# SBUF addresses of the weight rings and work regions: rings allocated last, one buffer padded from 392 to 512 bytes

## The chip, the cores and the metric

One core of one Trainium2 chip runs the whole program once. The metric is the device time of that execution in microseconds; lower is better. Each kernel is timed several times and the median is compared.

## What is computed

Two transformer-like blocks of two layers each, in float32, on one sequence of 256 tokens with 1024 features. The weights are each read once from HBM. Cut to what matters:

```python
# first block, DEPTH = 2
for layer in range(2):
    h = rms_norm(x, norm_mix[layer])
    x = x + hybrid_mixer(h, w_in[layer], ...)      # nine 1024x1024 projections, recurrence, conv, three more
    h = rms_norm(x, norm_ffn[layer])
    x = x + (swiglu(h, dense_w1, dense_w3, dense_w2) if layer == 0
             else moe_swiglu(h, router_w, expert_w1, expert_w3, expert_w2))   # 8 experts, top 2
x = rms_norm(x, final_norm)
# second block, DEPTH = 2
for l in range(2):
    x = x + 0.5 * rmsnorm(swiglu_ffn(rmsnorm(x, ...), ffn1_w_gu[l], ffn1_w_down[l]), ...)
    x = x + rmsnorm(mixing_sublayer(rmsnorm(x, ...), w_in[l], ...), ...)
    x = x + 0.5 * rmsnorm(swiglu_ffn(rmsnorm(x, ...), ffn2_w_gu[l], ffn2_w_down[l]), ...)
```

Every feed-forward has width 2816. An expert works on at most 128 gathered tokens, every other product on all 256.

## The kernel before, in words

All large weights are laid out ahead of time as one stream of **slabs**, each 128 partitions by 2048 float32 (1 MB). A slab goes through three rings of three slots each (`RING = 3`): SyncE's queue writes it from HBM into `raw` in two halves (`Sync.slabs`, L265), ScalarE rounds each half to float32r into `whi` (`Scalar.hi`, L301), VectorE computes the rest `wlo = raw - whi` (`Vector.lo`, L726), and TensorE multiplies (`Tensor.slab`, L1289 to L1291). The other operand is split in the same way into a high and a low part, and three products stand for one float32 product:

```python
            pe.matmul(ps, xh, k.whi[:, slot, cols], start=first, stop=False)
            pe.matmul(ps, xh, k.wlo[:, slot, cols], start=False, stop=False)
            mm = pe.matmul(ps, xl, k.whi[:, slot, cols], start=False, stop=last)
```

The first argument behind `ps` is the stationary operand (a weight load of 128 columns, 512 bytes a partition); the slab is the operand that streams past it, 512 columns or 2048 bytes a partition. Each of the three has a weight load of its own. So in the rows a matmul `ps<-whi,XH` streams `whi` past the stationary `XH`.

The stationary operands come in two places. `XH` and `XL` (the transposed, normalised input of a mixer or of a feed-forward's first product, for 256 tokens) are buffers of their own. `GH`/`GL` (the gated hidden activations, for the down product of a dense feed-forward), `GH_`/`GL_` (the same for an expert) and `XEH`/`XEL` (an expert's gathered input) lie in `region_z`, one region of 73,728 bytes a partition that the stages reuse by turns with different layouts. `region_b` is another such region, with the mixers' tables (`mcum`, L1387 and L1388, streams past `LFH` and `LFL`).

A slot of `raw` is written again once VectorE has read it; a slot of `whi` and `wlo` is written again once TensorE is done with its slab (the semaphores `dve_lo` and `pe_slab`). The order on every engine is written out in the code. In the down stage of an expert TensorE also gathers the next expert's tokens between slabs. The stages: mixer, dense feed-forward, mixer, the eight experts (each 22 slabs for the first products, the "up" stage, and 11 for the second, the "down" stage), then for each layer of the second block a feed-forward, a mixer, a feed-forward.

`Tiles.memory` allocates the buffers. Addresses are given out in the order of the calls, each rounded up to 32 bytes, beginning at byte 16,512 of each partition.

Of the kernel before, what the change touches and what calls it, by code (L numbers as in the profile page):

```python
# [8 lines left out]
F32R = mybir.dt.float32r  # L9
# [7 lines left out]
P = 128  # L17
# [20 lines left out]
SLAB = 2048  # L38
HALF = SLAB // 2
RING = 3  # L40
# [6 lines left out]
PCOLS = 2 * LCOLS + 2 * KT  # L47
# [11 lines left out]
class Tiles:  # L59
# [52 lines left out]
        return made  # L112

    def memory(self):
        self.raw = self.sb("raw", [P, RING, SLAB])
        self.whi = self.sb("whi", [P, RING, SLAB], F32R)
        self.wlo = self.sb("wlo", [P, RING, SLAB], F32R)
        self.X = self.sb("X", [P, NT, D])
        self.XN = self.sb("XN", [P, NT, D])
        self.XH = self.sb("XH", [P, KT, S], F32R)  # L120
        self.XL = self.sb("XL", [P, KT, S], F32R)
        self.ident = self.sb("ident", [P, P])
        self.small = self.sb("small", [P, 192])
        self.pcols = self.sb("pcols", [P, PCOLS])

        b = self.overlays("region_b", 6816, [
            ("mcum", [P, 12 * P], F32R),
            ("masks", [P, 7, P], U8),
            ("E1", [P, NT, 8, P], F32),
            ("KQ", [P, 2, 2 * S], F32),  # L130
            ("LFH", [P, 2, NT, P], F32R), ("LFL", [P, 2, NT, P], F32R),
            ("SM", [P, 2, NT, P], F32), ("SC", [P, 2, P], F32),
            ("ones1", [P, P], F32),
        ], [
            ("pad", [P, 3808], F32), ("mload", [P, 12 * P], F32), ("mask_load", [P, 7, P], F32),
        ], [
            ("RB", [P, NT, 4, S], F32),
            ("MP", [P, 4, 3 * P], F32),
            ("WS", [P, 4, P], F32),
            ("PW", [P, 4, 64], F32),  # L140
            ("pc2", [P, PC2], F32),
            ("gvb", [P, BW], F32),
            ("ones", [P, P], F32),
            ("GP", [P, D], F32),
        ], [
            ("pad2", [P, 4834], F32), ("bias_tmp", [P, 1028], F32),
        ])
        self.mcum, self.masks, self.E1, self.KQ, self.LFH, self.LFL, self.SM = (b[n] for n in ("mcum", "masks", "E1", "KQ", "LFH", "LFL", "SM"))
        self.SC, self.mload, self.RB, self.MP, self.WS, self.PW, self.pc2 = (b[n] for n in ("SC", "mload", "RB", "MP", "WS", "PW", "pc2"))
        self.gvb, self.ones, self.ones1, self.mask_load, self.GP, self.bias_tmp = (b[n] for n in ("gvb", "ones", "ones1", "mask_load", "GP", "bias_tmp"))  # L150

        n = 9 * SEG
        z = self.overlays("region_z", n, [("Z", [P, n], F32)], [
            ("GH", [P, FT, S], F32R), ("GL", [P, FT, S], F32R),
            ("SG", [P, 3, NT, S], F32), ("GN", [P, 3, NT, S], F32),
        ], [
            ("GH_", [P, FT, P], F32R), ("GL_", [P, FT, P], F32R),
            ("SG_", [P, 3, S], F32), ("GN_", [P, 3, S], F32),
            ("XEH", [P, KT, P], F32R), ("XEL", [P, KT, P], F32R),
            ("PM", [P, NT, P], F32),  # L160
            ("PT", [P, S], F32R),
            ("YH", [P, D], F32R), ("YL", [P, D], F32R),
            ("GB", [P, D], F32), ("RW", [P, KT, NE], F32), ("RWH", [P, KT, NE], F32R), ("RWL", [P, KT, NE], F32R),
            ("iota_", [P, P], F32), ("iota", [P, P], F32), ("ltri", [P, 3, P], F32), ("mo", [P, 512], F32),
        ], [
            ("Z2", [P, 12 * NT * CW], F32),
            ("HP", [P, 2, 30 + S], F32), ("CA", [P, 2, S], F32), ("CB", [P, 2, S], F32),
            ("QT", [P, 2, S], F32), ("KTT", [P, 2, S], F32), ("QI", [P, 2, S], F32),
            ("LG", [P, 4, S], F32), ("SCO", [P, 2, S], F32), ("WRK", [P, 2, S], F32), ("m8", [P, 16], F32),
        ])  # L170
        self.Z, self.GH, self.GL, self.SG, self.GN, self.GH_, self.GL_ = (z[n] for n in ("Z", "GH", "GL", "SG", "GN", "GH_", "GL_"))
        self.SG_, self.GN_, self.XEH, self.XEL, self.PM, self.PT, self.YH = (z[n] for n in ("SG_", "GN_", "XEH", "XEL", "PM", "PT", "YH"))
        self.YL, self.GB, self.RW, self.RWH, self.RWL, self.iota_, self.iota = (z[n] for n in ("YL", "GB", "RW", "RWH", "RWL", "iota_", "iota"))
        self.ltri, self.mo, self.Z2, self.HP, self.CA, self.CB, self.QT = (z[n] for n in ("ltri", "mo", "Z2", "HP", "CA", "CB", "QT"))
        self.KTT, self.QI, self.LG, self.SCO, self.WRK, self.m8 = (z[n] for n in ("KTT", "QI", "LG", "SCO", "WRK", "m8"))
        self.ps = self.stack.enter_context(self.nc.psum_tensor("ps", [P, 8, CW], F32))

        sm = self.small
        self.eps, self.rsin, self.nrs = sm[:, 0:1], sm[:, 20:22], sm[:, 24:26]
        self.ss, self.rs = sm[:, 8:10], sm[:, 16:18]  # L180
        self.oss, self.orn = sm[:, 32:48], sm[:, 48:64]
        self.gslot = sm[:, 64:65]
        self.lb_a = self.pcols[:, PCOLS - 2 * KT:PCOLS].rearrange("p (l c) -> p l c", l=2)
        self.lb_e, self.lb_s = sm[:, 128:144].rearrange("p (l c) -> p l c", l=2), sm[:, 120:128]
        self.lb = sm[:, 104:120].rearrange("p (l c) -> p l c", l=2)
# [1593 lines left out]
class Pool(Engine):  # L1779


    def start(self):
        pool, k = self.eng, self.k
        pool.dma_start(k.pcols[:], k.a["pcols"]).then_inc(*k.up("d_pcols", "pcols", 16))
        pool.memset(k.ident[:], 0.0).then_inc(*k.up("pool_step", "ident0"))
        pool.wait_ge(*k.at("ident0"))
        pool.affine_select(out=k.ident[:], in_=k.ident[:], compare_op=ALU.not_equal, fill=1.0, base=0, pattern=[[-1, P]],
                           channel_multiplier=1).then_inc(*k.up("pool_step", "ident"))
        pool.dma_start(k.mload[:], k.a["cum_sums"]).then_inc(*k.up("d_mload", "mload", 16))
        pool.dma_start(k.mask_load[:], k.a["level_masks"]).then_inc(*k.up("d_mask_load", "mask_load", 16))  # L1790
# [230 lines left out]
```

## Time and profile before

| | |
|---|---|
| median of 3 runs | 3147.94 us |
| the three runs | 3139.39, 3149.0, 3147.94 us |
| the profiled execution | 3144.32 us |
| its span, first to last instruction | 3142.6 us |
| mean granted share of TensorE's clock | 0.963 |

The span leaves out 1.7 us of the profiled execution's time. Every time worked out from the trace is one of this execution. A matmul's duration in the rows reaches past the start of the next, since matmuls are pipelined; what a matmul costs in a stream is the distance from its start to the next one's.

### The profile page before, as it was taken

How to read it: one execution, taken by the hardware profiler on the slowest of the kernel's cores; microseconds unless marked ns; L12 is line 12 of the kernel's file. 1: busy time of each engine (PE TensorE's matmuls, PEld its weight loads, DVE VectorE, ACT ScalarE, POOL GpSimd, SP SyncE). 2: the span in 40 equal slices, each digit the busy share in tenths (PEclk: the TensorE clock that was granted, in tenths of full speed). 3: DMA queues.
4: the chain of work that ended last, by engine and by line, in shares of the span. 5: the costliest groups of instructions: out<-in, count | busy, mean ns of one | idle time of the engine just before them, and what ended most of it. 6: DMA issues, size and time to landing. Idle time of an engine off the chain costs nothing.

```text
span 3142.6 us, 34313 instructions
## 1 busy us (share of the span) xinstructions
PE 2911.4 (93%) x13334; PEld 2381.7 (76%) x13334; DVE 2062.0 (66%) x2910; ACT 1696.8 (54%) x2271; POOL 33.3 (1%) x55
## 2 busy tenths in 40 slices
PE   8998899999887999999999989989899999898998
PEld 6887687788765778777777768777777787777786
DVE  5566654556664898888888865468655454587553
ACT  5655344555533777677767754355454443545543
POOL 0000000000001000000000000000000000000000
PEclk9998899999987999999999989999999999999999
DMA  6443355454343999999889965544455555444452
GB/s 221 144 134 121 121 188 174 157 165 135 125 134 124 337 347 332 321 328 334 315 310 335 348 231 187 174 141 154 150 171 175 173 184 170 148 161 147 163 185 101
DMA packets 173657, 633.63 MB, mean 202 GB/s; under 512 B 19520, under 2 KB 19520, under 8 KB 173488
## 3 DMA queue, kind: packets, MB, share of 16 engines
q1 hardware_dynamic: 170752, 621.88, 58.2%
q0 software_dynamic: 2736, 9.49, 0.9%
q8 instruction: 107, 1.75, 0.2%
q14 instruction: 62, 0.51, 0.1%
HBM read 629.20 MB, written 2.10 MB: 201 GB/s over the span
## 4 chain that ended last, share of the span: by engine, by line
PE 71%; DVE 16%; DMA 7%; ACT 5%; issue 1%; SPq 0%; DVEq 0%; ACTq 0%; POOLq 0%
PE ps L1289 21%; PE ps L1290 21%; PE ps L1291 21%; DMA raw<-in_W 7%; DVE wlo L726 7%; ACT whi L301 2%; PE ps L1401 2%; DVE CA L1165 2%; PE ps L1525 1%; PE ps L1478 1%; PE ps L1321 1%; DVE GL_ L932 0%; PE ps L1388 0%; PE ps L1387 0%; DVE XN L894 0%
## 5 line engine op out<-in xcount | busy, mean ns | idle before, releaser
L726 DVE TENSOR_TENSOR wlo<-raw,whi 128x1024 fp32r<-128x1024 f32 x1182 | 1394.5, 1223 | 583.5 <-ACT whi L301 575.7
L301 ACT ACTIVATE whi<-raw 128x1024 fp32r<-128x1024 f32 x1182 | 1200.7, 1058 | 638.5 <-PE ps L1291 558.7
L1289 PE MATMUL ps<-whi,XH 128*128 128x512 f32 (+1 forms) x2192 | 873.9, 399 | 43.1 <-DVE XL L744 18.4
L1291 PE MATMUL ps<-whi,XL 128*128 128x512 f32 (+1 forms) x2192 | 859.7, 392 | 0.0
L1290 PE MATMUL ps<-wlo,XH 128*128 128x512 f32 (+1 forms) x2192 | 859.4, 392 | 0.0
L1289 PEld LDWEIGHTS ps<-whi,XH 128*128 128x128 f32 x2192 | 418.4, 191 | 136.9 <-DVE XL L744 22.5
L1291 PEld LDWEIGHTS ps<-whi,XL 128*128 128x128 f32 x2192 | 417.3, 190 | 87.4
L1290 PEld LDWEIGHTS ps<-wlo,XH 128*128 128x128 f32 x2192 | 418.7, 191 | 82.4 <-issue 0.5
L1289 PE MATMUL ps<-whi,XEH 128*128 128x512 f32 x704 | 285.4, 405 | 2.6 <-DVE XEL L975 1.4
L1291 PE MATMUL ps<-whi,XEL 128*128 128x512 f32 x704 | 278.7, 396 | 0.0
L1290 PE MATMUL ps<-wlo,XEH 128*128 128x512 f32 x704 | 278.4, 395 | 0.0
L1289 PE MATMUL ps<-whi,GH 128*128 128x512 f32 x440 | 176.3, 401 | 18.7 <-DVE GN L922 11.6
L1290 PE MATMUL ps<-wlo,GH 128*128 128x512 f32 x440 | 175.6, 399 | 0.0
L1291 PE MATMUL ps<-whi,GL 128*128 128x512 f32 x440 | 175.5, 399 | 0.0
L1289 PE MATMUL ps<-whi,GH_ 128*128 128x512 f32 x352 | 148.1, 421 | 13.6 <-DVE GL_ L932 7.5
L1289 PEld LDWEIGHTS ps<-whi,XEH 128*128 128x128 f32 x704 | 132.5, 188 | 34.4 <-DVE wlo L726 4.6
L1291 PEld LDWEIGHTS ps<-whi,XEL 128*128 128x128 f32 x704 | 132.4, 188 | 31.6
L932 DVE TENSOR_TENSOR GL<-ps,GH 128x512 fp32r<-128x512 f32 x55 | 38.0, 692 | 178.9 <-ACT GH L480 178.9
L1290 PEld LDWEIGHTS ps<-wlo,XEH 128*128 128x128 f32 x704 | 132.7, 188 | 28.2
L480 ACT ACTIVATE GH<-ps 128x512 fp32r<-128x512 f32 x55 | 32.9, 598 | 223.6 <-PE ps L1478 223.6
L1290 PE MATMUL ps<-wlo,GH_ 128*128 128x512 f32 x352 | 141.6, 402 | 0.0
L1291 PE MATMUL ps<-whi,GL_ 128*128 128x512 f32 x352 | 141.5, 402 | 0.0
(358 smaller groups left out, 2475.8 us busy)
## 6 DMA issues: line engine op xcount, KB each, us to landing
raw<-in_W SPq DMA_DIRECT2D x1182, 512.0 KB, 5.3
GP<-in_ffn_post_g POOLq DMA_DIRECT2D x4, 512.0 KB, 3.9
X<-in_x SPq DMA_DIRECT2D x1, 1024.0 KB, 4.9
skew<-RB POOLq DMA_DIRECT2D x4, 256.0 KB, 2.8
RB<-skew POOLq DMA_DIRECT2D x8, 128.0 KB, 2.5
GP<-in_mix_post_g POOLq DMA_DIRECT2D x2, 512.0 KB, 3.9
out<-X SPq DMA_DIRECT2D x1, 1024.0 KB, 4.0
mload<-in_cum_sums POOLq DMA_DIRECT2D x1, 768.0 KB, 8.6
```

The lines of the kernel that those rows point to most:

```text
L301: act.activation(k.whi[:, slot, part], k.raw[:, slot, part], ACT.Copy).then_inc(*k.up("act_hi"))
L480: act.activation(GH[:, 2 * g:2 * g + 2, :], src, ACT.Copy).then_inc(*k.up("act_split", f"{T}.gh{g}"))
L726: dve.tensor_tensor(k.wlo[:, slot, part], k.raw[:, slot, part], k.whi[:, slot, part], ALU.subtract).then_inc(*k.up("dve_lo"))
L932: dve.tensor_tensor(GL[:, 2 * g:2 * g + 2, :], src, GH[:, 2 * g:2 * g + 2, :], ALU.subtract).then_inc(*k.up("dve_split", f"{T}.gl{g}"))
L1165: x = dve.scalar_tensor_tensor(out=CA[:, c, :], in0=HP[:, c, j:j + S], scalar=dw(c, j), in1=CA[:, c, :], op0=ALU.mult, op1=ALU.add)
L1289: pe.matmul(ps, xh, k.whi[:, slot, cols], start=first, stop=False)
L1290: pe.matmul(ps, xh, k.wlo[:, slot, cols], start=False, stop=False)
L1291: mm = pe.matmul(ps, xl, k.whi[:, slot, cols], start=False, stop=last)
L1321: mm = pe.transpose(bank[:, i * S + t * P:i * S + (t + 1) * P], src(2 * b + i, t), k.ident[:])
L1401: mm = pe.matmul(o, x, x, start=True, stop=True)
L1478: mm = pe.transpose(turned[:, fb, t * P:(t + 1) * P], GN[:, t, fb * P:(fb + 1) * P], k.ident[:])
L1525: mm = pe.matmul(k.ps[:, 6 + c // 4, (c % 4) * P:(c % 4 + 1) * P], k.XN[:, t, c * P:(c + 1) * P], k.PM[:, t, :], start=t == 0, stop=t == N ...
```

## The change

The three rings are allocated behind all other buffers instead of ahead of them, and `pcols` is made 128 columns wide instead of 98 (its load still fills 98). Nothing else changes: no instruction is added, removed or moved on any engine.

```diff
@@ def memory(self):
-        self.raw = self.sb("raw", [P, RING, SLAB])
-        self.whi = self.sb("whi", [P, RING, SLAB], F32R)
-        self.wlo = self.sb("wlo", [P, RING, SLAB], F32R)
         self.X = self.sb("X", [P, NT, D])
...
-        self.pcols = self.sb("pcols", [P, PCOLS])
+        self.pcols = self.sb("pcols", [P, 128])
...
+        self.raw = self.sb("raw", [P, RING, SLAB])
+        self.whi = self.sb("whi", [P, RING, SLAB], F32R)
+        self.wlo = self.sb("wlo", [P, RING, SLAB], F32R)
         self.ps = self.stack.enter_context(self.nc.psum_tensor("ps", [P, 8, CW], F32))
@@ def start(self):
-        pool.dma_start(k.pcols[:], k.a["pcols"]).then_inc(*k.up("d_pcols", "pcols", 16))
+        pool.dma_start(k.pcols[:, 0:PCOLS], k.a["pcols"]).then_inc(*k.up("d_pcols", "pcols", 16))
```

What the addresses (bytes in a partition) become, as the two built programs have them. Every ring slot, every 512-column piece of a slab and every 128-column piece of a stationary operand is a multiple of 512 bytes further on, so the remainder of the buffer is that of each operand.

| buffer | before | mod 512 | mod 64 | after | mod 512 | mod 64 |
|---|---|---|---|---|---|---|
| raw | 16,512 | 128 | 0 | 152,064 | 0 | 0 |
| whi | 41,088 | 128 | 0 | 176,640 | 0 | 0 |
| wlo | 65,664 | 128 | 0 | 201,216 | 0 | 0 |
| X, XN, XH, XL | from 90,240 | 128 | 0 | from 16,512 | 128 | 0 |
| mcum (region_b) | 124,704 | 288 | 32 | 51,072 | 384 | 0 |
| LFH, LFL (region_b) | 144,032 | 160 | 32 | 70,400 | 256 | 0 |
| GP (region_b) | 144,064 | 192 | 0 | 70,432 | 288 | 32 |
| region_z: Z, GH, GH_, XEH, GN, YH, PT | from 151,968 | 416 | 32 | from 78,336 | 0 | 0 |

So the rings and `region_z` do begin at multiples of 512 bytes after the change; `X`, `XN`, `XH`, `XL` keep their remainder of 128.

## Rows read from the trace of the kernel before

**Rows 1.** The page: span, busy shares, GB/s in 40 slices, chain's shares

```profile
span 3142.6 us, 34313 instructions
PE 2911.4 (93%) x13334; PEld 2381.7 (76%) x13334; DVE 2062.0 (66%) x2910; ACT 1696.8 (54%) x2271; POOL 33.3 (1%) x55
...
GB/s 221 144 134 121 121 188 174 157 165 135 125 134 124 337 347 332 321 328 334 315 310 335 348 231 187 174 141 154 150 171 175 173 184 170 148 161 147 163 185 101
...
PE 71%; DVE 16%; DMA 7%; ACT 5%; issue 1%; SPq 0%; DVEq 0%; ACTq 0%; POOLq 0%
```

**Rows 2.** The page's groups: line, engine, tiles, form, count, busy us, mean ns

```profile
L726 DVE TENSOR_TENSOR wlo<-raw,whi 128x1024 fp32r<-128x1024 f32 x1182 | 1394.5, 1223 | 583.5 <-ACT whi L301 575.7
L301 ACT ACTIVATE whi<-raw 128x1024 fp32r<-128x1024 f32 x1182 | 1200.7, 1058 | 638.5 <-PE ps L1291 558.7
L1289 PE MATMUL ps<-whi,XH 128*128 128x512 f32 (+1 forms) x2192 | 873.9, 399 | 43.1 <-DVE XL L744 18.4
...
L1289 PE MATMUL ps<-whi,XEH 128*128 128x512 f32 x704 | 285.4, 405 | 2.6 <-DVE XEL L975 1.4
...
L1289 PE MATMUL ps<-whi,GH 128*128 128x512 f32 x440 | 176.3, 401 | 18.7 <-DVE GN L922 11.6
...
L1289 PE MATMUL ps<-whi,GH_ 128*128 128x512 f32 x352 | 148.1, 421 | 13.6 <-DVE GL_ L932 7.5
```

**Rows 3.** Timeline, TensorE, stationary XH: a run's ends, 14 rows between

```profile
2130.50 0.39 PE L1289 MATMUL ps<-whi,XH 128*128 128x512 f32 x1
...
2133.90 0.39 PE L1289 MATMUL ps<-whi,XH 128*128 128x512 f32 x1
```

**Rows 4.** Timeline, stationary GH: a run's ends, 22 rows between

```profile
2017.06 0.40 PE L1289 MATMUL ps<-whi,GH 128*128 128x512 f32 x1
...
2022.43 0.40 PE L1291 MATMUL ps<-whi,GL 128*128 128x512 f32 x1
```

**Rows 5.** Timeline, stationary XEH: a run's ends, 11 rows between

```profile
1019.99 0.40 PE L1289 MATMUL ps<-whi,XEH 128*128 128x512 f32 x1
...
1022.79 0.40 PE L1289 MATMUL ps<-whi,XEH 128*128 128x512 f32 x1
```

**Rows 6.** Timeline, stationary XH behind loads of GN: ends, 7 rows between

```profile
2332.07 0.40 PE L1290 MATMUL ps<-wlo,XH 128*128 128x512 f32 x1
...
2333.93 0.39 PE L1289 MATMUL ps<-whi,XH 128*128 128x512 f32 x1
```

**Rows 7.** Timeline, mcum streaming past LFH and LFL, then XH

```profile
103.02 0.39 PE L1387 MATMUL ps<-mcum,LFH 128*128 128x512 f32 x1
...
104.64 0.40 PE L1388 MATMUL ps<-mcum,LFL 128*128 128x512 f32 x1
104.88 0.40 PE L1289 MATMUL ps<-whi,XH 128*128 128x512 f32 x1
```

**Rows 8.** Groups of one form: 128x512 from PSUM, into region_z and into XH, XL

```profile
L932 DVE TENSOR_TENSOR GL<-ps,GH 128x512 fp32r<-128x512 f32 x55 | 38.0, 692 | 178.9 <-ACT GH L480 178.9
L480 ACT ACTIVATE GH<-ps 128x512 fp32r<-128x512 f32 x55 | 32.9, 598 | 223.6 <-PE ps L1478 223.6
L311 ACT ACTIVATE XH<-ps 128x512 fp32r<-128x512 f32 x16 | 9.1, 596 | 35.7 <-PE ps L1321 35.7
L741 DVE TENSOR_TENSOR XL<-ps,XH 128x512 fp32r<-128x512 f32 x16 | 10.7, 688 | 2.7 <-ACT XH L311 2.5
```

**Rows 9.** Stretch, us, busy PE, PEld, DVE, ACT, POOL; clock, DMA share, GB/s

```profile
1000.50:1066.80 66.30, 64.81 (x290) 52.12 (x290) 59.35 (x67) 51.87 (x69) 0.00 (x0) 1.00 0.92 328
1309.90:1380.80 70.90, 67.99 (x299) 53.17 (x298) 62.94 (x71) 53.04 (x69) 0.00 (x0) 1.00 0.94 337
1380.80:1416.70 35.90, 34.94 (x167) 28.73 (x168) 27.07 (x27) 22.91 (x25) 0.00 (x0) 1.00 0.89 304
...
1000.00:1850.00 850.00, 819.07 (x3680) 658.83 (x3680) 718.99 (x757) 609.47 (x746) 0.93 (x2) 0.99 0.92 326
```

**Rows 10.** Waits in the experts' stretch: who for whom, us, times, longest

```profile
ACT whi L301 <- DMA raw<-in_W: 71.6, 116, 2.3
```

## The prediction

> **What bounds the kernel now.** I read the page's busy shares and chain first: TensorE is busy 93% of the span and is 71% of the chain that ended last [rows 1]. No instruction moves, so time can change only where an instruction or a DMA packet takes longer or shorter at its new address. The groups then say what there is most of: three lines of one product, 2192 matmuls a line on XH and XL, 704 on XEH and XEL, 440 on GH and GL, 352 on GH_ and GL_, and 1182 halves of a slab on ScalarE and on VectorE [rows 2]. Times three lines that is 6576 matmuls on XH and XL and 3 x (704 + 440 + 352) = 4488 on operands in region_z. Their mean durations of 399 to 421 ns reach over the next start, so the price of one has to be read as a distance between starts, in the timeline.
>
> There the reader should see two speeds for the same instruction. With XH stationary, 15 steps take 3.40 us, 226.7 ns each [rows 3]. With GH, 23 steps take 5.37 us, 233.5 ns [rows 4]; with XEH, 12 steps take 2.80 us, 233.3 ns [rows 5]. All stream the same ring slots, with 512 columns, at the same granted clock; the two slower ones come from different stages, one on 256 tokens and one on 128. What differs is the address of the stationary operand: XH begins at a remainder of 128 modulo 512 (0 modulo 64), region_z at 416 (32 modulo 64). 6.7 ns is 16 columns of 4 bytes at 2.4 GHz, 64 bytes, what one more 64-byte piece would be. Two more places fit. Behind four weight loads of GN (region_z), eight steps on XH take 1.86 us, 232.5 ns each, as if the stream had lost its place for a while [rows 6]. And mcum, at 32 modulo 64, streams at 1.62 us for 7 steps, 231.4 ns, and its last step, behind which an aligned XH is loaded, is 0.24 us [rows 7]. That last one matters: mcum and XH both lie below byte 131,072, so a high address does not explain it, and an offset of 32 does.
>
> VectorE and ScalarE show no such thing: the same 128x512 form takes 692 ns into GL and 688 into XL, and 598 into GH and 596 into XH [rows 8].
>
> **The change part by part.** After it the rings are at 0 modulo 512, region_z at 0, LFH and mcum at 256 and 384, XH and XL at 128 as before. Nothing that TensorE reads in bulk is left at 32 modulo 64.
>
> *Dense down products.* 3 x 440 = 1320 matmuls go from 233.4 to 226.7 ns: 1320 x 6.7 = 8.8 us. TensorE is the bound there, and the DMA moves 101 to 231 GB/s in the slices outside the experts, against 310 to 348 within [rows 1], so nothing else can take this back.
>
> *The experts.* 3 x (704 + 352) = 3168 matmuls, 21.2 us if all of it comes through. But here the DMA is 0.92 to 0.95 busy in the up stages [rows 9], and ScalarE waits 71.6 us for it in 116 places [rows 10]. An up stage is 22 slabs of 1.05 MB, 23.1 MB; at 348 GB/s, the highest slice of the page [rows 1], that is 66.3 us, and the fastest up stage takes 66.3 us, another 70.9 [rows 9]. So the lower bound for the up stages is a gain of nothing, with the wait for raw growing by what TensorE saves (2112 / 8 = 264 matmuls, 1.8 us an expert). The down stages have other work of TensorE between the slabs (35.9 us for 11 slabs at 304 GB/s [rows 9]): 1056 x 6.7 = 7.1 us comes through. Between 7 and 21 us I take the middle, 14: most steps of an up stage still go at TensorE's pace, and the ring holds three slabs of advance.
>
> *Smaller ones.* The lost place behind the loads of GN: 5.8 ns x 8 steps = 46 ns, at each of the 55 groups of the dense feed-forwards (GL is written 55 times [rows 8]), 2.6 us; nothing to 3. The mcum products, 2 layers x 4 pairs of heads x 2 x 8 = 128 matmuls, from 231.4 to 226.7 ns: 0.6 us. The wider pcols costs no instruction. GP and a few tables go from 0 to 32 modulo 64; by rows 8 that costs VectorE at most some 4 ns an instruction. The slab halves on VectorE and ScalarE stay at 1223 and 1058 ns [rows 2]: 0, or 4 ns either way, behind TensorE.
>
> *XH and XL.* 6576 matmuls, aligned to 64 on both sides before and after: 0. This is the largest unknown, since the trace has no pair of operands at different multiples of 64 and none at 0 modulo 512; the two bounds are priced as rivals below.
>
> The sum: 8.8 + 14 + 2.6 + 0.6 = 26.0 us off the profiled execution's 3144.3, 3118. That execution lies 3.6 us under the median of the runs shown and inside their spread of 9.6 us; I forecast 3119.
>
> What the Trainium skill says speaks against this. Its page "SBUF — State Buffer", section "Operand start alignment", only asks that an operand start at a multiple of its element size, calls that a matter of legality and not of speed, and says its runs timed nothing; its "Specifications" give 16-byte cachelines, of which 128 and 416 are both multiples, so by these nothing would change and the sum would be 0. The trace disagrees, with 226.7 against 233.5 ns for one form. The page "TensorE: Matmul & The Clock Gate", "Back-to-back issue gap", gives N/2.4 + 2.5 ns, 215.8 for 512 columns, and its step on LDWEIGHTS says that the next load takes no SBUF bandwidth from the running matmul; the trace shows 226.7 at best, 10.9 more.
>
> **The rivals.**
>
> *A: no change.* The 6.7 ns come from something else that GH and XEH share, as that they are rewritten by ScalarE and VectorE while TensorE works, and the address is a coincidence. Against it: GH and XEH are written at quite different rates and have the same step, and mcum, which nobody writes, has it too [rows 4, 5, 7]. Then 3144. Chance 0.14.
>
> *B: slower.* What counts is the place of the two operands to each other, or the height of the address. Before, the ring and XH had the same remainder, 128; after, they are 0 and 128, and the rings lie above byte 152,064. The step of the XH products then rises by the same 6.7 ns: 6576 x 6.7 = 44.1 us, less the 26.0: 3162. It decides once more than some 3,900 of the 6,576 are hit (26.0 / 0.0067). For it: mcum and LFH differ by 128 modulo 512, as the ring and XH will, and step by 231.4 ns. Against it: they are also both at 32 modulo 64, and for height, mcum and the XH loaded behind it both lie low and are as slow [rows 7]. Chance 0.10.
>
> *C: much faster.* The remaining 13.4 ns above 512 columns at 2.4 GHz (213.3) are the price of the remainder of 128, and go where both operands begin at 0 modulo 512. Then region_z's products step by 213.3 ns: 1320 x 20.1 = 26.5 us dense, 1056 x 20.1 = 21.2 in the experts' down stages, some 7 in the up stages, which the DMA bounds at 66.3 us, and 3 as above: 58 us, 3086. If the XH products gained by the ring's 0 alone, a further 6576 x 13.4 = 88 us, below 3000. No row here speaks for either. Chance 0.13 together, a third of it for the second.
>
> *D: the DMA gains too.* raw goes from 128 to 0 modulo 256. Were an up stage's packets a few per cent shorter, the rest of the 21.2 us and some of the 71.6 us of waits would come back: some 7 + 8 = 15 us more, 3103. No row shows a packet at 0 modulo 256. The Trainium skill's "DMA: Bandwidth & Descriptors", "How a descriptor splits into AXI transactions", makes a read that begins off a 256-byte boundary cost one more transaction; raw is the side that is written, and HBM's side does not move, so the rule as it stands gives 0; no run here shows it. Chance 0.05, inside the forecast's side.
>
> **How the numbers follow.** The forecast has 0.58, and by itself a range of 3105 to 3133: the experts' 7 to 21 us and the runs' spread of some 5 us either way. With A, D and that part of C without XH it reaches from 3083 to 3150; outside are B and the rest of C, about 0.15, and a little of each tail. Within 0.3%, 9.4 us (about what a measurement of this kernel tells from no change), lie A and a sliver of the forecast: 0.15. Slower is B: 0.10. Faster is the rest: 0.75.
>
> **What would show it.** Right: in the changed kernel's timeline the steps on GH, GH_ and XEH are 227 ns, those on XH stay 227, also behind the loads of GN, and mcum's fall to 227; the dense down stages are shorter by 1.8 us each; an expert's down stage by 0.9; the up stages by 0 to 1.8, with ScalarE's wait for raw growing from 71.6 us. Wrong: steps on GH still 233 (A), on XH above 230 (B), any step near 213 (C), or ScalarE's wait for raw falling while TensorE is faster (D). What would make the number wrong with all of this right is the part that the experts' DMA takes back, and the half-rate stretches of TensorE's clock, which fall differently in each execution.

## The result, and the profile after

The changed kernel is slower: 3162.07 us median against 3145.84 us before, ratio 1.007 with a 95% interval of 1.0048 to 1.0092. The forecast was 3119 us, 0.9% faster. Rival B, slower by the products on XH, had named 3162. One of the eight executions of each kernel was in a slow state (5840 and 5685 us); the ratio leaves these two out.

The starts of TensorE's products show why. The first fence is the timeline of the changed kernel on XH, 23 rows left out; the second on GH, 25 left out; the third on XEH, 10 left out.

```profile
2141.30 0.39 PE L1289 MATMUL ps<-whi,XH 128*128 128x512 f32 x1
...
2146.87 0.39 PE L1289 MATMUL ps<-whi,XH 128*128 128x512 f32 x1
```

```profile
2030.00 0.39 PE L1289 MATMUL ps<-whi,GH 128*128 128x512 f32 x1
...
2035.89 0.39 PE L1291 MATMUL ps<-whi,GL 128*128 128x512 f32 x1
```

```profile
1024.75 0.39 PE L1289 MATMUL ps<-whi,XEH 128*128 128x512 f32 x1
...
1027.24 0.40 PE L1291 MATMUL ps<-whi,XEL 128*128 128x512 f32 x1
```

24 steps on XH take 5.57 us, 232.1 ns each, where they took 226.7 [rows 3]. 26 steps on GH take 5.89 us, 226.5 ns, where they took 233.5 [rows 4]; 11 on XEH take 2.49 us, 226.4 ns, where they took 233.3 [rows 5]. The two groups have changed places, and the one that lost is the larger, 6576 matmuls against 4488.

The page's groups show the same in the mean durations, which reach over the next start: XH from 399 to 403 ns, GH from 401 to 397; the other two engines are as in [rows 2].

```profile
L726 DVE TENSOR_TENSOR wlo<-raw,whi 128x1024 fp32r<-128x1024 f32 x1182 | 1394.2, 1221 | 589.0 <-ACT whi L301 581.2
L301 ACT ACTIVATE whi<-raw 128x1024 fp32r<-128x1024 f32 x1182 | 1202.1, 1058 | 657.7 <-PE ps L1291 558.1
L1289 PE MATMUL ps<-whi,XH 128*128 128x512 f32 (+1 forms) x2192 | 883.6, 403 | 40.6 <-DVE XL L744 18.7
...
L1289 PE MATMUL ps<-whi,GH 128*128 128x512 f32 x440 | 174.5, 397 | 18.7 <-DVE GN L922 11.7
```

Where in the program: busy time by stretch, cut at the first slab product of each stage (columns: stretch, us, busy PE, PEld, DVE, ACT, POOL, granted clock, DMA share, GB/s). The stages are the first mixer with the dense up products, the dense down products, the experts, and the last layer's mixer with its up products; before, then after.

```profile
19.00:514.70 495.70, 466.68 (x2224) 389.04 (x2224) 301.06 (x589) 253.16 (x380) 0.00 (x0) 0.96 0.46 151
514.70:586.00 71.30, 66.56 (x285) 53.19 (x285) 30.76 (x30) 24.14 (x31) 0.00 (x0) 0.96 0.49 162
...
1000.50:1860.50 860.00, 822.75 (x3696) 662.11 (x3696) 723.27 (x764) 613.85 (x756) 3.80 (x6) 0.98 0.92 324
...
2705.40:3066.80 361.40, 334.65 (x1544) 273.79 (x1544) 242.68 (x332) 182.03 (x245) 5.83 (x5) 0.97 0.49 162
```

```profile
18.90:524.20 505.30, 476.22 (x2224) 389.80 (x2224) 301.25 (x589) 253.57 (x380) 0.00 (x0) 0.96 0.45 148
524.20:592.30 68.10, 62.91 (x285) 51.65 (x285) 30.77 (x30) 24.17 (x30) 0.00 (x0) 1.00 0.51 170
...
1010.80:1869.50 858.70, 815.00 (x3697) 663.62 (x3697) 721.45 (x764) 613.26 (x756) 3.97 (x6) 0.97 0.92 325
...
2724.80:3094.10 369.30, 344.10 (x1545) 276.69 (x1545) 242.62 (x332) 182.17 (x245) 5.83 (x5) 0.96 0.49 158
```

All six stages on XH together go from 1888.5 to 1922.3 us (+33.8), the five dense down stages from 362.9 to 356.1 (-6.8), the experts from 860.0 to 858.7 (-1.3): 25.7 us together, and the two spans (3168.2 and 3142.6) differ by 25.6. The medians lie 16 us apart and the ratio says 22; the profiled execution of the changed kernel was one of its slower ones.

The experts hardly gain although their matmuls are faster. ScalarE's wait for slabs has grown from the 71.6 us of [rows 10] (first line), while its wait for TensorE (second line) fell from 68.1 us:

```profile
ACT whi L301 <- DMA raw<-in_W: 89.7, 145, 2.0
ACT whi L301 <- PE ps L1291: 59.4, 63, 1.9
```

### The profile page after: what moved, and what is told of

It is laid out like the page before. It is cut to its first block, busy times and chain, and to the rows that moved or that the text cites. A ratio compares the mean times of both kernels' runs of the same rounds, so it can differ in the third digit from the quotient of the medians.

```text
span 3168.2 us, 34313 instructions
## 1 busy us (share of the span) xinstructions
PE 2933.1 (93%) x13334; PEld 2387.5 (75%) x13334; DVE 2060.3 (65%) x2910; ACT 1697.3 (54%) x2271; POOL 33.5 (1%) x55
## 4 chain that ended last, share of the span: by engine, by line
PE 69%; DVE 16%; DMA 8%; ACT 4%; issue 1%; SPq 0%; DVEq 0%; ACTq 0%; POOLq 0%
PE ps L1289 21%; PE ps L1291 20%; PE ps L1290 20%; DMA raw<-in_W 8%; DVE wlo L726 8%; PE ps L1401 2%; DVE CA L1165 2%; ACT whi L301 2%; PE ps L1525 1%; PE ps L1478 1%; DVE GL_ L932 1%; DVE GN_ L924 1%; DVE X L982 1%; PE ps L1321 1%; PE ps L1387 0%
## 5 line engine op out<-in xcount | busy, mean ns | idle before, releaser
L726 DVE TENSOR_TENSOR wlo<-raw,whi 128x1024 fp32r<-128x1024 f32 x1182 | 1394.2, 1221 | 589.0 <-ACT whi L301 581.2
L301 ACT ACTIVATE whi<-raw 128x1024 fp32r<-128x1024 f32 x1182 | 1202.1, 1058 | 657.7 <-PE ps L1291 558.1
L1289 PE MATMUL ps<-whi,XH 128*128 128x512 f32 (+1 forms) x2192 | 883.6, 403 | 40.6 <-DVE XL L744 18.7
L1290 PE MATMUL ps<-wlo,XH 128*128 128x512 f32 (+1 forms) x2192 | 870.0, 397 | 0.0
L1291 PE MATMUL ps<-whi,XL 128*128 128x512 f32 (+1 forms) x2192 | 869.9, 397 | 0.0
L480 ACT ACTIVATE GH<-ps 128x512 fp32r<-128x512 f32 x55 | 32.8, 597 | 232.4 <-PE ps L1478 232.4
```

What stands on the lines that cost most here:

```text
L301: act.activation(k.whi[:, slot, part], k.raw[:, slot, part], ACT.Copy).then_inc(*k.up("act_hi"))
L480: act.activation(GH[:, 2 * g:2 * g + 2, :], src, ACT.Copy).then_inc(*k.up("act_split", f"{T}.gh{g}"))
L726: dve.tensor_tensor(k.wlo[:, slot, part], k.raw[:, slot, part], k.whi[:, slot, part], ALU.subtract).then_inc(*k.up("dve_lo"))
```

## The experiments

The theories are told in the expectations. Where a step is given without a fence it is the mean distance between starts of consecutive products of one family (XH with XL, GH with GL, and so on) in that kernel's trace, distances outside 215 to 250 ns left out. R, the theory that came out of the changed kernel's trace, says that a product is fast where its streaming and its stationary operand have the same remainder.

**One part alone, and both sides aligned alike.** `match128` is the kernel before with

```diff
+        self.gap = self.sb("gap", [P, 56])          # 224 bytes, unused, ahead of region_z
```

> The kernel before with one unused buffer of 224 bytes ahead of region_z: rings, XH, XL and region_z all at a remainder of 128 modulo 512. Theory R (a matmul is fast, 226.7 ns, where the operand that streams and the stationary one loaded behind it have the same remainder, and takes 5 to 7 ns more where they differ): steps 227 ns on XH and on GH, XEH, GH_; by the 3 x 440 dense products 8.8 us and some 3 us of smaller ones faster, and 0 to 21 us in the experts; 3120 to 3135 us. Theory A64 (only an offset of 32 modulo 64 costs, and the rings' high place made the changed kernel slow): the same here. Theory H (rings or region_z high are slow): region_z still high, steps on GH stay 233, 3146.

Measured: 3133.34 us, ratio to before 0.9964 (0.9948 to 0.9979). Steps: 227.2 ns on XH, 226.9 on GH, 227 to 228.6 on XEH and GH_. That is what R said of the steps. The time is 9 us lower by the medians and 11 by the ratio, near the slow end of the 3120 to 3135 us expected. Theory H falls: region_z lies as high as before (152,192) and is fast.

`match0` is the changed kernel with

```diff
+        self.gap = self.sb("gap", [P, 96])          # 384 bytes ahead of X
+        self.gap2 = self.sb("gap2", [P, 32])        # 128 bytes ahead of region_z
```

> The changed kernel with unused buffers of 384 bytes ahead of X and 128 ahead of region_z: rings, XH, XL and region_z all at 0 modulo 512, rings last. Theory R: steps 227 ns everywhere, 3120 to 3135 us, as match128. Theory H (the rings' high place): XH steps stay at 233 as in the changed kernel, 3155 to 3165. If a start at a multiple of 512 were of use in itself, steps under 227 and a time under match128's.

Measured: 3131.7 us, ratio 0.9963 (0.995 to 0.9977), steps of 227.2 ns on XH and 227.0 on GH. The same as `match128`, though the rings are last and rings, XH, XL and region_z are at 0 instead of 128. So neither the rings' height nor the multiple of 512 does anything that shows; some 30 us separate it from the changed kernel, by 512 bytes of padding.

`last_only` is the changed kernel with pcols at 98 columns again:

```diff
-        self.pcols = self.sb("pcols", [P, 128])
+        self.pcols = self.sb("pcols", [P, PCOLS])
```

> The half of the change that moves the rings behind, with pcols at 98 columns: rings and region_z at 416, XH at 128. Theory R: steps on GH and XEH 227 although both operands are at 32 modulo 64, steps on XH 233, time as the changed kernel, 3160 within 8. Theory A64: all steps 233, some 25 to 40 us slower than the changed kernel. Theory H: XH 233, GH 227 (no distinction from R).

Measured: 3169.22 us, ratio 1.0081 (1.0063 to 1.01). Its timelines, first on XH (17 rows left out), then on XEH (17 left out):

```profile
1875.51 0.40 PE L1290 MATMUL ps<-wlo,XH 128*128 128x512 f32 x1
...
1879.71 0.39 PE L1290 MATMUL ps<-wlo,XH 128*128 128x512 f32 x1
```

```profile
1012.13 0.40 PE L1290 MATMUL ps<-wlo,XEH 128*128 128x512 f32 x1
...
1016.22 0.39 PE L1290 MATMUL ps<-wlo,XEH 128*128 128x512 f32 x1
```

On XH 18 steps take 4.20 us, 233.3 ns each, with XH at 128 and the ring at 416; on XEH 18 take 4.09 us, 227.2 ns, with both at 416. Both operands are at 32 modulo 64 in the fast pair, which ends theory A64, the one that the prediction rested on.

`pad_only` is the kernel before with the wider pcols alone (rings first):

> The half of the change that pads pcols to 512 bytes, rings first: rings and XH at 128, region_z at 0. Theory R: XH 227, GH and XEH 231 to 234, time as before, within 5 us. Theory A64: GH and XEH 227, 12 to 30 us faster than before.

Measured: 3140.12 us, ratio 0.9997 (0.9985 to 1.0008); steps of 227.3 ns on XH and 232.4 on GH, with region_z at 0 modulo 512. A start at a multiple of 512 bytes brings next to nothing beside a ring at 128 (the slow step falls from 233.3 to 232.4). Of the two halves of the change, the move of the rings makes the whole loss.

**Which distances.** Three kernels set the distance from the ring's remainder family by family, by unused columns ahead of XH, ahead of XL and at the head of region_z's layouts; one run each. `map1`:

> The kernel before with padding that sets the remainder of each stationary operand, modulo 512, to the ring's 128 plus: XH, XL 256; GH, GL 64; GH_, GL_ 192; XEH, XEL 32. Theory R512 (only an equal remainder modulo 512 is fast): every step 231 to 234 ns. Theory R256: XH 227, the others slow. Theory R64 (equal modulo 64 would do) is out already by the pairs at 128. If the price grew with the distance, XEH (32) would be near 227 and XH (256) highest.

`map2`:

> The same with other distances: XH, XL 64; GH, GL 256; GH_, GL_ 96; XEH, XEL 480 (32 below the ring). Theory R512: every step 231 to 234 ns. Theory R256: GH 227. XH at 64 beside GH at 64 in the other kernel says whether the price is that of the distance or of the stage; a time some 35 us over before with XH off, as in the changed kernel.

`map3`:

> The kernel before with other distances from the ring's 128: XH 0 but XL 64; GH, GL 192; GH_, GL_ 160; XEH, XEL 64. Theory next (the price belongs to the matmul that runs while the odd operand is loaded): the second product (wlo with XH, behind it XL is loaded) steps by 233 ns and more, the third (whi with XL, behind it XH) by 227. Theory own (it belongs to the matmul whose own weights lie apart): the third is the slow one, the second 227. Distance 192 was in between in the experts, 226 to 232; if that was the distance, GH shows 229 to 230 here, if it was the stage, 227 or 233. 160 and 64: 231 to 235.

Measured, with the other kernels (distance: stationary less streaming operand, modulo 512). A step is the mean of a family; in brackets the lowest and highest of its three products, where they differ by over 1 ns beside a distance other than 0:

| distance | where | step, ns |
|---|---|---|
| 0 | XH before, pad_only, match128, match0, dense_match; GH after, match128, match0, last_only, dense_match | 226.9 to 227.3 |
| 0 | XEH and GH_ in match128, match0, last_only | 227.7 to 228.1 |
| 0 | XEH and GH_ after | 228.2, 229.7 |
| 32 | XEH in map1 | 233.1 |
| 64 | GH in map1, XH in map2, XEH in map3 | 233.3, 233.3, 233.5 |
| 96 | GH_ in map2 | 234.3 (233.1 to 235.0) |
| 128 | XH after | 232.8 |
| 160 | GH_ in map3 | 233.1 (231.6 to 236.2) |
| 192 | GH in map3; GH_ in map1 | 229.0 (227.4 to 230.3); 229.6 (228.4 to 231.8) |
| 224 | XH in last_only; XEH in dense_match | 233.3, 233.3 |
| 256 | XH in map1, GH in map2 | 227.2, 226.8 |
| 288 | GH before | 233.3 |
| 384 | GH in pad_only | 232.4 |
| 480 | XEH in map2 | 233.1 |

The timeline of `map1` on XH, 256 off the ring, 17 rows left out:

```profile
2126.86 0.39 PE L1294 MATMUL ps<-whi,XH 128*128 128x512 f32 x1
...
2130.93 0.39 PE L1294 MATMUL ps<-whi,XH 128*128 128x512 f32 x1
```

18 steps in 4.07 us, 226.1 ns. Theory R512 falls and R256 stands: what has to agree is the remainder modulo 256, as far as multiples of 32 bytes were tried. Elsewhere the price is some 5 to 7 ns and doesn't grow with the distance, but at 192 it is some 2 ns on the mean. The single times go with it: `map1` with XH fast 3137.42 us, `map2` with XH slow 3177.07, `map3` 3163.27.

One family does not fit the rule: GH_ in the changed kernel agrees with the ring and still steps by 229.7 ns. The trace says where. In the seven down stages in which TensorE also gathers the next expert's tokens (`ps<-PM,XN`) the mean is 230.0 to 230.5 ns, in the eighth, without gathers, 227.2. Between two gathers of the changed kernel, where XN is at 128 and all else here at 0, 8 steps take 1.85 us, 231.3 ns each (first fence, 7 rows left out); in `match0`, where XN too is at 0, 1.81 us, 226.3 ns (second fence, 7 left out).

```profile
1101.35 0.40 PE L1289 MATMUL ps<-whi,GH_ 128*128 128x512 f32 x1
...
1103.20 0.40 PE L1291 MATMUL ps<-whi,GL_ 128*128 128x512 f32 x1
```

```profile
1091.34 0.39 PE L1291 MATMUL ps<-whi,GH_ 128*128 128x512 f32 x1
...
1093.15 0.39 PE L1293 MATMUL ps<-whi,GL_ 128*128 128x512 f32 x1
```

So what TensorE did before a run of products has a part in their step, beside their own two addresses. How it does so stays open.

In `map3` XH agrees with the ring and XL lies 64 off. The steps are 228.7 ns (whi with XH), 229.4 (wlo with XH, behind it XL is loaded) and 235.0 (whi with XL). Theory next asked for 233 on the second, theory own for 227 on the first two and 233 on the third; own is the nearer, but the first two are not clean. Which load it is that collides is not settled.

**Where the experts' gain goes.** Of every slab of the experts, the thin kernels load the first 512 columns of each half only, and so leave out half of the weights:

```diff
+                if MOE_BASE <= self.n < MOE_BASE + NE * FF_SLABS:
+                    part = slice(h * HALF, h * HALF + HALF // 2)
                 sp.dma_start(k.raw[:, slot, part], k.a["W"][base + self.n, :, part])
```

> The kernel before, but of every slab of the experts only half the columns are loaded (the first 512 of each half of 1024), the rest of the slot keeps what it held; all else runs as before. Theory DMA (in the experts the DMA sets the pace and takes back what TensorE saves): with half the bytes the experts' stretch shortens by itself, 5 to 30 us off before, and the pair with thin_match then differs by more than the full-load pair does. Theory none (the experts have another bound): time as before, and the same distance of the pair as at full load.

> match128 (all stationary operands at the ring's remainder) with the same half loads in the experts. Theory DMA: under thin_before by the full 4488 x 6.7 ns = 30 us, within 6, 21 of them in the experts. Theory none: under it by some 10 us, as match128 is under before.

Measured: `thin_before` 3124.77 us, ratio 0.9945 (0.9924 to 0.9965); `thin_match` 3099.92 us, 0.9857 (0.9835 to 0.9879). The pair lies 24.9 us apart, the pair with full loads (before and `match128`) 9.4. In the traces the experts take 841.3 and 827.2 us, 14.1 apart, where at full load they took 860.0 and 858.8. Theory DMA asked for 30 us within 6 and 21 of them in the experts; the first came just inside, the second fell short. The longest waits in that stretch behind POOL's, of `match128` and then of `thin_before`, with ScalarE's wait for raw at the end:

```profile
DVE wlo L727 <- ACT whi L302: 95.4, 136, 1.9
ACT whi L302 <- DMA raw<-in_W: 88.0, 151, 2.7
ACT whi L302 <- PE ps L1292: 60.7, 64, 1.7
```

```profile
ACT GH_ L482 <- PE ps L1480: 94.2, 88, 1.7
DVE wlo L728 <- ACT whi L303: 91.1, 152, 2.4
ACT whi L303 <- PE ps L1293: 90.9, 139, 2.7
...
ACT whi L303 <- DMA raw<-in_W: 1.7, 1, 1.7
```

With half the bytes ScalarE's wait for raw is all but gone: 1.7 us in `thin_before`, 1.0 in `thin_match`. At full load it is 88.0 us in `match128`, 16 more than the 71.6 before [rows 10].

`dense_match` is `match128` with the experts' operands moved off again:

```diff
+            ("pz_", [P, 56], F32),                  # 224 bytes ahead of GH_, GL_, ..., XEH, XEL
             ("GH_", [P, FT, P], F32R), ("GL_", [P, FT, P], F32R),
```

> match128 with the experts' operands alone (GH_, GL_, XEH, XEL and what lies behind them) moved off the ring's remainder by 224 bytes again; the dense down products keep the match. Theory DMA (the experts' 21 us are taken back by the wait for slabs): time as match128, 3133 within 5, ratio to before 0.995 to 0.998, with steps of 233 ns on XEH and GH_. If the match in the experts brought its 21 us, or half of it, the time would be 3140 or more, as before.

Measured: 3132.5 us, ratio 0.9956 (0.9941 to 0.9972), with steps of 233.3 ns on XEH and 226.9 on GH; ScalarE's wait for raw is 78.0 us. The same time as with the match: by the two intervals the match in the experts is worth 5 us at most, so the 21 us, and half of them, are excluded. At full load it makes no difference that shows where the experts' operands lie.

## Why the prediction was wrong

- **The two speeds, and their price: right.** Steps near 227 and near 233 ns come back in trace after trace, and which of the two a family has follows the addresses. Rival A is out.
- **The step that failed: "what differs is the address of the stationary operand".** The prediction read the slow pairs as an offset of 32 modulo 64, one more 64-byte piece, and found the same sum in columns. It is the relation of the two operands: they have to agree modulo 256. In `last_only` XEH and the ring are both at 32 modulo 64 and step by 227.2 ns; in `pad_only` GH and the ring are both at 0 modulo 64 and step by 232.4. Every slow pair of the trace before had both properties, an offset of 32 and a disagreement; mcum with LFH [rows 7] disagrees too (288 and 160) and could not tell them apart, as was noted under rival B and then given 0.10. The changed kernel brought region_z and the rings together at 0 and left XH at 128.
- **"XH and XL", 6576 matmuls at 0: the term that this got wrong.** It measured +33.8 us by the stages. From the steps, 6576 x 5.6 ns = 37 us; part of the products does not follow one of its own kind.
- **Rival B: right, and its 3162 partly by luck.** It took 44.1 less 26.0 us, 18.1; the traces show 33.8 less 8.1, 25.7, and the ratio says 22.
- **Rival C: out.** With both operands at 0 modulo 512 in `match0` the steps are 227, not 213.
- **Dense down products, 8.8 us: nearly right.** The stages show 6.8 after and 10.2 in `match128` (362.9 to 352.7).
- **The experts, 14 us of 21.2: wrong.** Their stretch went from 860.0 us to 858.7 in the changed kernel and 858.8 in `match128`, but from kernel to kernel it scatters by more than that: 854.1 us in `match0` and 863.2 in `last_only`, where the operands agree, 857.0 in `pad_only` and 859.4 in `dense_match`, where they do not. No gain stands out. By the steps of `match128` TensorE saved 2112 x 5.0 + 1056 x 5.5 ns = 16.4 us, less than 21.2. With half the bytes 14.1 us come through.
- **The experts' lower bound, 7 us from the down stages: too high.** The eight up stages together take 549.6 us before and 551.6 in `match128`: what they save is all waited for, since the same queue fills the same three slots. The eight down stages take 310.4 and 307.2. At full clock (2.4 GHz) a down stage does get shorter, from 35.8 or 35.9 us to 35.1 or 35.2, near the 0.9 us forecast. But of the first seven, five in `match128` begin with a stretch at the half rate (1.2 GHz), against two before, and then take 36.6 to 36.8 us at a granted clock of 0.95 or 0.96. The clock falls within 1.4 us of the stage's first product, behind waits of TensorE of 2 to 3 us in the 6 us ahead of it. Whether the shorter step brings this about isn't shown: `thin_match` has one such stage in seven. One stage before and two of `match128` (columns as in the fences by stretch above):

```profile
1066.80:1102.70 35.90, 34.95 (x166) 28.71 (x167) 26.83 (x26) 23.20 (x25) 0.00 (x0) 1.00 0.89 309
```

```profile
1166.60:1203.40 36.80, 35.87 (x167) 29.82 (x168) 26.93 (x26) 22.96 (x25) 0.00 (x0) 0.95 0.86 294
1270.30:1305.40 35.10, 34.17 (x166) 28.62 (x167) 26.87 (x26) 22.98 (x25) 0.00 (x0) 1.00 0.90 311
```

- **The lost place behind GN, 2.6 us: nothing.** In `match128`, where GN agrees with the ring, the steps behind its loads are as slow as in [rows 6]: 6 in 1.39 us, 231.7 ns.

```profile
2323.89 0.60 PE L1479 MATMUL ps<-ident,GN 128*128 128x128 f32 x4
...
2324.56 0.39 PE L1291 MATMUL ps<-wlo,XH 128*128 128x512 f32 x1
...
2325.95 0.39 PE L1291 MATMUL ps<-wlo,XH 128*128 128x512 f32 x1
```

- **The mcum products, 0.6 us: nothing.** Their two operands stay 128 apart, since they move together, and step by 233.1 ns after 232.3 before.
- **VectorE and ScalarE unmoved: right,** 1221 and 1058 ns after 1223 and 1058. D is out: with raw at 0 modulo 256 the experts' packets of 4 KB take a median of 159 ns, as before, and ScalarE's wait for raw did not fall.
- **The range, 3083 to 3150:** it left out B. A rival whose condition the change fulfils (the ring's remainder moves, XH's stays) and that no row excludes was worth more than one in ten.

Left open: whether it is the load for the product itself or for the next one that collides, why 192 costs less than the other distances, why products stay slow behind those on GN and, in the changed kernel, behind the gathers, and what the 13.4 ns above 512 columns are, which no address here removed.

## What to carry to other kernels

Give the operand that streams through TensorE and the one that is loaded for it the same start address modulo 256 bytes; this is shown for float32r with a new load for every product. Here a gap of 224 bytes ahead of one region took 0.36% off, and an alignment "to 512" of some buffers and not of others cost 0.7%. When two groups of the same instruction run at different speeds, list for each every property in which it differs, relations between operands too, and ask of a layout change which relations it breaks rather than which buffers it aligns. And a saving on TensorE in a stretch where the DMA is nearly full may be worth nothing, as here at 0.92 busy; a run with fewer bytes tells.

## What the runs showed of the hardware

A 128x512 float32r product with a load of its own steps by 226.7 ns where both operands agree modulo 256 bytes, and by 232 to 234 ns on the mean where they do not (229 to 230 at a distance of 192), whatever their own alignment (0, 128 or 416 modulo 512 are equally fast in agreement) and wherever they lie between bytes 16,512 and 226,304 of the partition. Among other products, those on GN or the gathers, the step can stay at 231 ns even in agreement. The Trainium skill's page "TensorE: Matmul & The Clock Gate" ("Step-by-step: what each phase is for") gives the next load a read port of its own that takes nothing from the running product; the traces disagree, since the price depends on how the two addresses stand to each other. For float32 products over 128 columns no such price shows: the four on GN with ident step by 108.5 ns before, 288 apart, and by 108.4 in `match128`, 0 apart.
